# A one-core decoder block: when GpSimd writes its ones, how row factors are spread, and the layout of the recurrence's output

## The reference

```python
mod = silu(c) @ w_ada + b_ada                      # shift1, scale1, gate1, shift2, scale2, gate2
h = rms_norm(x, norm1_g) * (1 + scale1) + shift1
proj = h @ w_in                                    # q_lat, a_k, a_v, k_idx, w_idx, b_q, b_f, b_i, b_g, gate_a, gate_b
out_a = dsa_attention(...)                         # indexer scores, the best 128 keys a query, 8 heads of 64
o_b = hgrn2_chunkwise(silu(b_q), b_f, b_i, lb)     # gated linear recurrence, 4 heads of 128
out_b = rms_norm(o_b, hgrn_o_norm_g) * silu(b_g)   # norm over the 128 values of a head, token by token
merged = sigmoid(gate_a) * (out_a @ w_proj_a) + sigmoid(gate_b) * (out_b @ w_proj_b)
x = x + gate1 * (merged @ w_out)
h2 = rms_norm(x, norm2_g) * (1 + scale2) + shift2
x = x + gate2 * (square(relu(h2 @ w_mlp1 + b_mlp1)) @ w_mlp2 + b_mlp2)
```

## Time and profile before

| what | value |
|---|---|
| runs | 807.06, 807.44, 808.18 us; median 807.44 |
| profiled execution, span | 805.9 us (the trace gives no other time for it; the median is 1.5 us above it) |
| TensorE busy | 795.4 us, 99% of the span |
| VectorE, ScalarE, GpSimd busy | 448.3, 320.9, 214.6 us |
| TensorE's waits for others, in total | 7.2 us in four places |

### The profile page before, as it was taken

The page is one execution under the profiler, slowest core; times in us unless marked ns, Lnnn a source line. Parts: engine busy times, 40 slices in busy tenths (PEclk is TensorE's granted clock), DMA queues, the critical chain, the costliest instruction groups (busy, mean ns, idle before and its releaser), DMA issues.

```text
span 805.9 us, 10816 instructions
## 1 busy us (share of the span) xinstructions
PE 795.4 (99%) x4004; PEld 654.3 (81%) x4004; DVE 448.3 (56%) x801; ACT 320.9 (40%) x497; POOL 214.6 (27%) x124
## 2 busy tenths in 40 slices
PE   8999998999999999999999999999999999999998
PEld 6887877888888876667889998888888888888886
DVE  6965996667987856786966789421111222220000
ACT  5574523443443266564432554442122244332110
POOL 5024307200000000000002056444544434444440
PEclk9999998999999999999999999999999999999999
DMA  9942203221121222445747236323233222233320
GB/s 351 370 136 100 80 25 131 79 78 53 54 79 53 79 78 84 143 147 180 214 153 253 86 117 222 104 100 106 81 104 103 80 104 94 88 104 104 95 88 26
DMA packets 27623, 95.22 MB, mean 118 GB/s; under 512 B 3009, under 2 KB 3393, under 8 KB 27586
## 3 DMA queue, kind: packets, MB, share of 16 engines
q1 hardware_dynamic: 27296, 94.51, 34.5%
q10 hardware_dynamic: 290, 0.20, 0.1%
HBM read 92.61 MB, written 2.10 MB: 118 GB/s over the span
## 4 chain that ended last, share of the span: by engine, by line
PE 97%; DVE 1%; ACT 1%; POOL 0%; issue 0%; DMA 0%; DVEq 0%; POOLq 0%; ACTq 0%
PE bank L1365 17%; PE bank L1367 17%; PE bank L1366 17%; PE bank L1414 4%; PE bank L1566 4%; PE bank L1568 4%; PE bank L1567 4%; PE bank L1590 2%; PE bank L1548 2%; PE bank L1762 2%; PE bank L1763 2%; PE bank L1764 2%; PE bank L1550 2%; PE bank L1549 2%; PE bank L1723 1%; PE bank L1843 1%
## 5 line engine op out<-in xcount | busy, mean ns | idle before, releaser
L396 POOL TENSOR_TENSOR w_lo<-w_raw,w_hi 128x1024 fp32r<-128x1024 f32 x77 | 192.2, 2499 | 254.3 <-ACT w_hi L456 254.3
L456 ACT ACTIVATE w_hi<-w_raw 128x1024 fp32r<-128x1024 f32 (+2 forms) x126 | 131.3, 1043 | 135.4 <-PE bank L1367 119.7
L1365 PE MATMUL bank<-h_hi,w_hi 128*128 128x512 f32 x328 | 129.1, 394 | 3.5 <-POOL w_lo L396 3.5
L1366 PE MATMUL bank<-h_lo,w_hi 128*128 128x512 f32 x328 | 128.5, 392 | 0.0
L1367 PE MATMUL bank<-h_hi,w_lo 128*128 128x512 f32 x328 | 128.4, 391 | 0.0
L1365 PE MATMUL bank<-u_hi,w_hi 128*128 128x512 f32 x256 | 99.6, 389 | 0.0
L1366 PE MATMUL bank<-u_lo,w_hi 128*128 128x512 f32 x256 | 99.6, 389 | 0.0
L1367 PE MATMUL bank<-u_hi,w_lo 128*128 128x512 f32 x256 | 99.6, 389 | 0.0
L1315 DVE TENSOR_TENSOR sqr_u<-relu_u 128x512 f32<-128x512 f32 x32 | 32.8, 1025 | 87.4 <-ACT relu_u L828 87.4
L1365 PEld LDWEIGHTS bank<-h_hi,w_hi 128*128 128x128 f32 x328 | 62.1, 189 | 16.3 <-POOL w_lo L396 3.6
L1367 PEld LDWEIGHTS bank<-h_hi,w_lo 128*128 128x128 f32 x328 | 62.2, 190 | 13.1
(11 more groups left out here) (267 smaller groups left out, 1430.1 us busy)
## 6 DMA issues: line engine op xcount, KB each, us to landing
w_raw<-in_units SPq DMA_DIRECT2D x117, 512.0 KB, 3.3
ada_raw<-in_ada SPq DMA_DIRECT2D x16, 512.0 KB, 11.0
ada_even<-in_ada SPq DMA_DIRECT2D x16, 512.0 KB, 4.3
ada_odd<-in_ada SPq DMA_DIRECT2D x16, 512.0 KB, 4.4
w_raw<-in_units SPq DMA_DIRECT2D x8, 448.0 KB, 10.9
xT<-in_xt SPq DMA_DIRECT2D x4, 512.0 KB, 5.5
out<-xT SPq DMA_DIRECT2D x7, 256.0 KB, 4.1
w_raw<-in_units SPq DMA_DIRECT2D x1, 256.0 KB, 5.5
```

The lines of the kernel that those rows point to most:

```text
L396: nc.gpsimd.tensor_tensor(w_lo[:, s], w_raw[:, s], w_hi[:, s].bitcast(F32), ALU.subtract).then_inc(lo_ready, 1)
L456: nc.scalar.activation(w_hi[:, s, 0:width], w_raw[:, s, 0:width], ACT.Copy).then_inc(hi_ready, 1)
L1365: mm(bank[b][:], w_hi[:, slot, j], rhs_hi(i), start=f, stop=False)
L1366: mm(bank[b][:], w_hi[:, slot, j], rhs_lo(i), start=False, stop=False)
```

## The change

GpSimd splits units 18 to 21 first, then writes the ones for two heads, then splits units 22 to 25. The recurrence's output products exchange their operands, so that bank 5 has tokens on the partitions (128 tokens of each of four blocks) and a head's 128 values along the free axis. The squares of a token then lie along the free axis, and VectorE sums them (`o_sum`); ScalarE takes the root of that in place; VectorE multiplies bank 5 with the inverse root of each token into `o_nat` (`o_scale`); TensorE turns `o_nat` by four transposes into bank 7 (`turn_out`, in the place of `spread`); and VectorE multiplies with gain and gate in one operation. The sums on TensorE (`out_sums`) are gone. `row_spread` and `half_spread` use transposes of the broadcast column in place of fp32 products with the identity.

```diff
@@ -139,7 +140,7 @@
         q_sig = place("q_sig", RL + 8 * KB, [P, T])
         hg_t = place("hg_t", RL + 10 * KB, [P, T])
         osq = place("osq", RL + 12 * KB, [P, T])
-        o_diag = place("o_diag", RL + 12 * KB, [P, TB, P])
+        o_nat = place("o_nat", RL + 12 * KB, [P, T])
         hg_s = place("hg_s", RL + 14 * KB, [P, 3, P])
         sig_b = place("sig_b", RL + 16 * KB, [P, KC, T])
         sq_o = place("sq_o", RA + 16 * KB, [P, 2, T])
@@ -211,7 +212,7 @@
         ks_ready, ks_turned, kn_ready, kv_done, s_ready, o_done = (
             sem("ks_ready"), sem("ks_turned"), sem("kn_ready"), sem("kv_done"), sem("s_ready"),
             sem("o_done"))
-        odiag_ready, o_spread = sem("odiag_ready"), sem("o_spread")
+        on_ready, o_turned = sem("on_ready"), sem("o_turned")
         osq_ready, osq_summed, ort_ready, o_ready, obhi_ready, ob_ready = (
             sem("osq_ready"), sem("osq_summed"), sem("ort_ready"), sem("o_ready"), sem("obhi_ready"),
             sem("ob_ready"))
@@ -409,11 +410,12 @@
             def e_ones(h):
                 nc.gpsimd.memset(hg("e", h), 1.0).then_inc(e_ready, 1)
 
+            split_range(U_B + WS, U_F)
             pool.wait_ge(rel_used, 3 * IH)
             pool.wait_ge(qsq_summed, 1)
             e_ones(0)
             e_ones(1)
-            split_range(U_B + WS, U_F + WS)
+            split_range(U_F, U_F + WS)
             for h in range(2, BH):
                 pool.wait_ge(ks_ready, h - 1)
                 e_ones(h)
@@ -640,14 +642,13 @@
 
                 act.wait_ge(o_done, h + 1)
                 if h:
-                    act.wait_ge(o_spread, h)
+                    act.wait_ge(o_turned, h)
                 nc.scalar.activation(osq[:], bank[5][:], ACT.Square).then_inc(osq_ready, 1)
 
             def o_root(h):
 
                 act.wait_ge(osq_summed, h + 1)
-                nc.scalar.activation(ORS, bank[7][:, 0:TB], ACT.Sqrt, scale=1.0 / P,
-                                     bias=EPSC).then_inc(ort_ready, 1)
+                nc.scalar.activation(ORS, ORS, ACT.Sqrt, scale=1.0 / P, bias=EPSC).then_inc(ort_ready, 1)
 
             def head_out(h):
 
@@ -1057,21 +1058,31 @@
                 v.tensor_tensor(hg_g[:] if j == BH - 1 else g, g, bT[:, 2 * BH + j], ALU.mult
                                 ).then_inc(silu_ready, 1)
 
+            def o_sum(h):
+
+                dve.wait_ge(osq_ready, h + 1)
+                if h:
+                    dve.wait_ge(on_ready, h)
+                v.tensor_reduce(ORS, osq[:].rearrange("p (b n) -> p b n", b=TB), AXES.X, ALU.add
+                                ).then_inc(osq_summed, 1)
+
             def o_scale(h):
 
                 dve.wait_ge(ort_ready, h + 1)
                 step(v.reciprocal(ORS, ORS))
-                v.tensor_tensor(o_diag[:], ident[:].unsqueeze(1).to_broadcast([P, TB, P]),
-                                ORS.unsqueeze(2).to_broadcast([P, TB, P]), ALU.mult).then_inc(odiag_ready, 1)
+                if h:
+                    dve.wait_ge(o_turned, h)
+                v.tensor_tensor(o_nat[:].rearrange("p (b n) -> p b n", b=TB),
+                                bank[5][:].rearrange("p (b n) -> p b n", b=TB),
+                                ORS.unsqueeze(2).to_broadcast([P, TB, P]), ALU.mult).then_inc(on_ready, 1)
 
             def head_out(h):
 
-                dve.wait_ge(o_spread, h + 1)
+                dve.wait_ge(o_turned, h + 1)
                 dve.wait_ge(silu_ready, h + 1)
                 g = hg_g[:] if h == BH - 1 else bT[:, 3 * BH + h]
-                step(v.scalar_tensor_tensor(out=hg_t[:], in0=bank[5][:], scalar=col[:, V_OG + h:V_OG + h + 1],
-                                            in1=g, op0=ALU.mult, op1=ALU.mult))
-                v.tensor_tensor(hg_t[:], bank[7][:], hg_t[:], ALU.mult).then_inc(o_ready, 1)
+                v.scalar_tensor_tensor(out=hg_t[:], in0=bank[7][:], scalar=col[:, V_OG + h:V_OG + h + 1],
+                                       in1=g, op0=ALU.mult, op1=ALU.mult).then_inc(o_ready, 1)
 
             def head_out_lo(h):
 
@@ -1132,6 +1143,8 @@
                     step(v.tensor_tensor(ef, ef, hg_ends(h, H), ALU.mult))
                     if l == 0 and h:
                         states(h - 1)
+                    if l == 2 and h:
+                        o_sum(h - 1)
                     if l == 3 and h:
                         o_scale(h - 1)
                     if l <= 4:
@@ -1206,6 +1219,8 @@
                             out=pr[:, e, OFF_Q[qb]:OFF_Q[qb] + n], in0=bank[LOGIT_BANK[p > 0][t % 4]][:, 0:n],
                             in1=score[:, qb, 0:n], scale=q_root[:, qb, 2 * p + e:2 * p + e + 1], scalar=-TAKEN, op0=ALU.add, op1=ALU.min,
                             accum_out=smx[:, 1, 2 * p + e, qb:qb + 1]).then_inc(logit_masked, 1)
+                        if p == 0 and t == 3:
+                            o_sum(BH - 1)
                     if p == 0:
                         o_scale(BH - 1)
                     for t, qb, e in heads(p):
@@ -1380,8 +1395,8 @@
             def row_spread(b0, r):
 
                 for b in range(TB):
-                    end = mm(bank[b0][:, b * P:(b + 1) * P], r[:, b:b + 1].to_broadcast([P, P]), ident[:],
-                             start=True, stop=True)
+                    end = nc.tensor.transpose(bank[b0][:, b * P:(b + 1) * P], r[:, b:b + 1].to_broadcast([P, P]),
+                                              ident[:])
                 return end
 
             def idle_products(count):
@@ -1639,28 +1654,24 @@
                 pe.wait_ge(lvl_taken, 6 * h + 6)
                 pe.wait_ge(s_ready, (TB - 1) * (h + 1))
                 if h:
+                    pe.wait_ge(on_ready, h)
+                for b in range(TB):
+                    t = slice(b * P, (b + 1) * P)
+                    end = mm(bank[5][:, t], hg_at[:, h % 2, t], i_nat[:, b, h * P:(h + 1) * P], start=True,
+                             stop=b == 0)
+                    if b:
+                        end = mm(bank[5][:, t], hg("q", h)[:, t], hg_s[:, b - 1], start=False, stop=True)
+                end.then_inc(o_done, 1)
+
+            def turn_out(h):
+
+                pe.wait_ge(on_ready, h + 1)
+                if h:
                     pe.wait_ge(o_ready, h)
                 for b in range(TB):
                     t = slice(b * P, (b + 1) * P)
-                    end = mm(bank[5][:, t], i_nat[:, b, h * P:(h + 1) * P], hg_at[:, h % 2, t], start=True,
-                             stop=b == 0)
-                    if b:
-                        end = mm(bank[5][:, t], hg_s[:, b - 1], hg("q", h)[:, t], start=False, stop=True)
-                end.then_inc(o_done, 1)
-
-            def out_sums(h):
-
-                pe.wait_ge(osq_ready, h + 1)
-                for b in range(TB):
-                    end = mm(bank[7][:, b:b + 1], osq[:, b * P:(b + 1) * P], ones[:, 0:1], start=True, stop=True)
-                end.then_inc(osq_summed, 1)
-
-            def spread(h):
-
-                pe.wait_ge(odiag_ready, h + 1)
-                for b in range(TB):
-                    end = mm(bank[7][:, b * P:(b + 1) * P], ones[:], o_diag[:, b], start=True, stop=True)
-                end.then_inc(o_spread, 1)
+                    end = nc.tensor.transpose(bank[7][:, t], o_nat[:, t], ident[:])
+                end.then_inc(o_turned, 1)
 
             pe.wait_ge(v_ready, TB)
             level(-1, 0)
@@ -1678,14 +1689,12 @@
                     sum_squares(8, 1, twins)
                 level(1, h)
                 fill(4)
-                if h:
-                    out_sums(h - 1)
-                else:
+                if h == 0:
                     sum_squares(9, 1, twins)
                 level(2, h)
                 fill(4)
                 if h:
-                    spread(h - 1)
+                    turn_out(h - 1)
                 else:
                     sum_squares(10, 1, twins)
                 level(3, h)
@@ -1770,13 +1779,12 @@
             outputs(BH - 1)
             gate_blocks(KC, 6, 8)
             logits(0, 0, 4)
-            out_sums(BH - 1)
             gate_blocks(KC + 1, 0, 1)
             logits(0, 4, 6)
             gate_blocks(KC + 1, 1, 2)
             logits(0, 6, 8)
             gate_blocks(KC + 1, 2, 8)
-            spread(BH - 1)
+            turn_out(BH - 1)
             for p in range(1, PAIRS):
                 j = KC + 2 * p
 
@@ -1861,8 +1869,8 @@
                 if x:
                     pe.wait_ge(lin_evac, E_O + KC)
                 for b in (2 * x, 2 * x + 1):
-                    end = mm(bank[6 - x][:, b * P:(b + 1) * P], ORS[:, b:b + 1].to_broadcast([P, P]), ident[:],
-                             start=True, stop=True)
+                    end = nc.tensor.transpose(bank[6 - x][:, b * P:(b + 1) * P], ORS[:, b:b + 1].to_broadcast([P, P]),
+                                              ident[:])
                 end.then_inc(orow_spread, 1)
 
             for m in range(M_H, KC):
```

(1 more changed line is left out.)

## The result

The changed kernel takes 797.85 us (median of 4 runs, 797.11 to 798.20), the kernel before 807.81 (4 runs, 807.06 to 808.37): a ratio of 0.9879, 95% interval 0.9865 to 0.9893. The forecast was 798.2, a ratio of 0.9886 to the 807.44 it started from. In a later comparison the changed kernel was run again, 798.18 against 807.28 (0.9885, 0.9869 to 0.9902).

A forecast was written before the change was run, and what follows sets the result against it. TensorE's instruction stream and its few stops were taken to bound the kernel. 5.80 + 3.15 + 0.45 + 0.44 - 0.60 = 9.24 us off the 805.9 us span gave 796.7, plus 1.5 for runs: 798.2 us, range 796.0 to 801.2.

The forecast's parts named there:

- Ones later: GpSimd's memsets of ones behind the splits of units 18 to 21: TensorE's stop and low clock go, 5.80 us gained.
- Index-key row factors: Row spread for the index keys by transposes, in TensorE's stream: 0.45 us gained.
- half spreads: Second norm's row factors, two halves of two blocks each, by transposes: 0.44 us gained.
- The start: Row spread at the kernel's start by transposes: hidden behind VectorE's conditioning dot product, 0 gained.
- Heads 0 to 2: Recurrence output: sums leave TensorE, transposes replace spread products, less waits for the scale; 0.69 + 1.23 + 1.23 = 3.15 us gained.
- Head 3: Last head: ScalarE's root waits for VectorE's reduction behind four masked logits; TensorE stands 2.0 us, 0.6 us lost.
- The clock rival: Head 3's new 2.0 us stop takes TensorE's clock down once: 2.3 us lost again, 800.5 us; chance 0.24.
- The sum: All terms over the whole kernel: 9.24 us gained, span 796.7 us, runs 798.2 us.
- The slower case: Clock falls in head 3's stop and stays down through attention; with 30 us at half clock 813 us; chance 0.03.

The follow-up runs named there:

- experiment 5: Changed kernel with VectorE's sum of head 3's squares moved ahead of the first attention pair's masked logits; 796.82 us, ratio 0.9869 to the kernel before.
- experiment 6: Changed kernel with head 3's reduction of squares done twice (798.62 us, ratio 0.9898) or four times (801.99 us, ratio 0.9929).
- rows alone: Kernel before with only the row and half spreads issued as transposes instead of fp32 products; 807.12 us against 807.24, ratio 0.9995.
- the recurrence alone: Changed kernel with GpSimd's order and the row spreads put back, so only the recurrence's output differs from before; 803.88 us, ratio 0.9952.

## Why the prediction was right, and where it was off

*Ones later, 5.80 forecast.* 5.78 measured alone in the profiled execution. The reading behind it, 12.19 - 6.39 from the copies and not the 3.48 of the stop, holds; nothing was late next. What one trace could not show is that this is the dearer of two prices: the runs of before at a mean clock of 0.998 are 1.1 us shorter on average than those at 0.996.

*Index-key row factors, 0.45; half spreads, 0.44.* 0.45 to 0.47, and 0.5. The start: 0.16, where 0 was forecast; the spread ended just behind VectorE's product, not under it. What the prediction did not see is that the first of these would have been worth less beside the stop (0.21 and 0.36, by two executions of the code with the stop).

*Heads 0 to 2, 0.69 + 1.23 + 1.23 = 3.15.* 3.03. Head to head it was 33.62, 33.21 and 32.11 us before and is 32.96, 32.04 and 30.91: 0.66, 1.17 and 1.20. The wait for the scale was forecast at 0.66, 0.12 and 0.12 and is 0.66, 0.10 and 0.10. The rest of the small miss is the transposes: 0.49 behind a wait, not 0.43. The reduction takes 0.68 to 0.69 us, forecast 0.67 from MAX8; the estimate of 0.53 from the Trainium skill ("VectorE: DVE Perf Modes", the perf-mode tier table) is lower than the row. In the loop its length is hidden, as said.

*Head 3, -0.60.* The mechanism is right and the size is off: -0.23. The chain came as written: the root waits for the reduction (1.46), the first exponential is 1.48 later (forecast 1.56), the restart 0.54 (forecast 0.65), experiment 5 removes all of it. Two things are missing. One is small: the restart comes 0.54 later, where the sum has 0.60. The other is a gain that the prediction named and priced at nothing: "The output step on VectorE is one operation instead of two." Before, that step's second operation reached through ScalarE's queue to TensorE's second transposes of probabilities; without it 0.31 us go behind the restart, whatever the length of the stop (experiment 5). This is read from the order of the rows; no run changes the output step alone.

*The clock rival (0.24).* It did not come in at a stop of 1.60 nor, in three runs of four, of 2.32, and came in at 3.76 with the price that was named. Its mechanism deserved a place in the range. That the 2.0 forecast would have left the clock up is likely by these stops, and no more than that.

*The sum.* 9.24 forecast, 9.5 from A to the end in the trace, 9.96 and 9.10 by the medians of two comparisons. That 798.2 met 797.85 so closely is partly luck. The span was forecast at 796.7 and is 795.6, with 0.76 of the difference ahead of A. The 1.5 us added for the runs was too little: it set the median of three runs against the span of one execution of the costlier kind, while every run whose own span is recorded is 1.9 to 2.5 us above it (the changed kernel's median lies 2.25 above its profiled span). The two errors, -1.1 and +0.75, go against each other. The errors of the terms (-0.12, +0.37, +0.1) are smaller than what separates the two comparisons.

*The slower case* asked for a clock that stays down through attention. Even after the long stop of experiment 6 it was back within 7 us.

## What to carry to other kernels

Take the price of a stop from the distance of two landmarks around it, not from the idle time alone: here 5.8 against 3.5, because the clock falls and stays down for a while. Then look at the mean clock of every run: the price can differ from one execution to the next, here by some 1.1 us. A small edit in front of such a stop can be worth less than alone, here 0.21 to 0.36 of 0.45. When work moves from the engine that bounds to one with slack, look first at its place in the new engine's queue: the same 0.68 us reduction cost 1.35 us behind four masked logits and nothing in front of them. And follow an operation that goes away through the queues behind it, even on an engine with slack: here it gave TensorE 0.3 us, two engines further on.

## What the runs showed that I had not expected

The clock's fall and return were not tied to the moment at which TensorE stopped or began again. With rows alone TensorE stopped and restarted 0.52 us earlier than before, yet the mean clock of the microsecond from 121 was 0.56 against 0.58, and the return lay at 128.0 in both (with the recurrence alone, which stopped when before did, at 0.68 and 128.2). A stop of 1.60 us left the clock up, while before it fell 1.4 us after the last work, and with the sum four times 2.6 us after it (289.0 to 291.6, from the 0.89 of the window). With a stop of 2.32 it seems to have fallen in one run of four. So the length of a stop alone does not say whether the clock falls, nor for how long; what does was not tested here.
